# Moving the sample group's projections, attention and pooling from the first to the third group of a decoder step

## The reference, cut to what matters

```
z = x @ w_in                                  # pool 512 | q 512 | k 128 | v 128 | gates 2 x 1024
p_out, pool_state = pool_mixer(p, pool_prev, ...)   # windows 2, 4, 8, 16
o, k_state, v_state = attn(q, k, v)           # samples: kk = concat([ck, k]), vv = concat([cv, v])
m = g_pool * (p_out @ w_up_pool) + g_attn * (o @ w_up_attn)
x = layer_norm(alpha * x + m @ w_out)
idx, gate = top 16 of 128 x 128 experts, 8 heads    # product keys
x = layer_norm(alpha * x + sum_k gate_k * gelu(x . u[idx_k]) * v[idx_k])
```

## Time and profile before

| | |
|---|---|
| median of three runs | 3105.41 us (3104.44 to 3107.35) |
| the profiled execution | 3107.77 us, span 3105.9 us |
| busy, share of the span | PE 85%, DVE 74%, POOL 40%, ACT 31% |
| DMA | 1255.14 MB, mean 404 GB/s; q0 (gathers) 1107.36 MB, q1 (SP) 139.92 MB |
| chain that ended last | DMA 44%, PE 32%, DVE 16% |

### The profile page before, as it was taken

One profiled execution on the slowest core, in us unless ns is written; L12 is line 12 of the kernel. 1 busy time (PEld: TensorE's weight loads), 2 busy tenths in 40 slices (PEclk: granted clock), 3 DMA queues, 4 the chain that ended last, 5 costly groups with the idle time before them and its releaser, 6 DMA issues.

```text
span 3105.9 us, 31170 instructions
## 1 busy us (share of the span) xinstructions
PE 2643.5 (85%) x8204; PEld 1435.9 (46%) x8204; DVE 2297.3 (74%) x4977; ACT 955.6 (31%) x3100; POOL 1233.7 (40%) x1060
## 2 busy tenths in 40 slices
PE   8889999899998888999999879899877777676665
PEld 7866676555544444544444436434322222222222
DVE  2479668888866676888997676788878877666666
ACT  2124323333432232322444221433322322222222
POOL 0123433343443444334444444433454444544542
PEclk9989999999999999999999999999999998988988
DMA  9999999999999999999999999999999999999996
GB/s 284 250 414 417 384 417 419 419 419 419 420 420 418 420 408 412 411 402 414 404 408 380 418 420 420 421 420 418 419 421 421 421 421 422 421 421 422 421 421 259
DMA packets 203654, 1255.14 MB, mean 404 GB/s; under 512 B 31100, under 2 KB 34764, under 8 KB 67920
## 3 DMA queue, kind: packets, MB, share of 16 engines
q0 software_dynamic: 152064, 1107.36, 86.3%
q1 hardware_dynamic: 48656, 139.92, 12.5%
q10 hardware_dynamic: 2760, 5.88, 0.5%
HBM read 1247.39 MB, written 5.79 MB: 403 GB/s over the span
## 4 chain that ended last, share of the span: by engine, by line
DMA 44%; PE 32%; DVE 16%; issue 4%; ACT 2%; DVEq 1%; POOL 1%; ACTq 0%; POOLq 0%
DMA ring<-in_uv,idx 38%; PE acc L1103 15%; PE wide L1084 9%; DVE ring L1382 7%; DMA wring<-in_uv,idx 3%; PE wide L1301 3%; DVE acc_v L1393 2%; DMA wring<-in_w_q 2%; PE wide L1272 2%; DVEq L1366 1%; PE wide L1200 1%; DMA bias<-in_uv,idx 1%; POOL ring L848 1%; PE wide L1182 1%; ACT diag L893 1%
## 5 line engine op out<-in xcount | busy, mean ns | idle before, releaser
L848 POOL DMA_INDIRECT ring<-in_uv,idx x906 | 1054.3, 1164 | 1560.8 <-PE acc L1103 1044.8
L1103 PE MATMUL acc<-ring,diag 128*128 128x512 f32 (+1 forms) x2808 | 1373.1, 630 | 271.7 <-ACT diag L893 258.0
L1382 DVE CUSTOM_DVE_ANT_0 ring<-ring,xb 128x1024 f32<-128x1024 f32 x906 | 1097.0, 1225 | 469.5 <-DMA ring<-in_uv,idx 433.7
L1103 PEld LDWEIGHTS acc<-ring,diag 128*128 128x128 f32 (+1 forms) x2808 | 540.6, 199 | 975.2 <-issue 956.8
L879 ACT ACTIVATE hgelu<-hdot 128x2 f32<-128x2 f32 x528 | 107.2, 203 | 1723.3 <-DVE hdot L1382 1722.8
L1084 PE MATMUL wide<-xm,wring 128*128 128x256 f32 (+5 forms) x2352 | 608.6, 408 | 19.5 <-DMA wring<-in_w_q 18.4
L1084 PEld LDWEIGHTS wide<-xm,wring 128*128 128x128 f32 x2352 | 429.0, 197 | 214.0 <-issue 107.8
L893 ACT ACTIVATE diag<-ident,hw 128x128 f32<-128x128 f32 x813 | 294.3, 396 | 47.9 <-PE acc L1103 5.0
L1393 DVE SCALAR_TENSOR_TENSOR acc_v<-ring,hw,acc_v 128x1024 f32<-128x1024 f32 x204 | 262.1, 1285 | 38.2 <-ACT hw L882 17.9
L882 ACT ACTIVATE hw<-hgelu,gate 128x1 f32<-128x1 f32 x1056 | 253.6, 287 | 37.0 <-issue 0.7
L1301 PE MATMUL wide<-wring,big 128*128 128x256 f32 (+1 forms) x536 | 124.8, 379 | 0.0
(11 more groups left out here) (242 smaller groups left out, 1992.7 us busy)
## 6 DMA issues: line engine op xcount, KB each, us to landing
wring<-in_w_a SPq DMA_DIRECT2D x141, 512.0 KB, 7.9
wring<-in_w_q SPq DMA_DIRECT2D x64, 576.0 KB, 8.1
ring<-in_uv,idx POOLq DMA_INDIRECT x906, 20.7
ring<-in_w_a SPq DMA_DIRECT2D x27, 512.0 KB, 8.2
out_y_prompt<-xb ACTq DMA_DIRECT2D x7, 512.0 KB, 7.9
att<-in_ln_g SPq DMA_DIRECT2D x4, 512.0 KB, 12.1
att<-in_ln_b SPq DMA_DIRECT2D x4, 512.0 KB, 15.2
xm<-in_xT SPq DMA_DIRECT2D x1, 1536.0 KB, 10.5
```

What stands on the lines that cost most here:

```text
L848: pool.indirect_dma_start(slot(s), None, uv, bass.IndirectOffsetOnAxis(ap=idx[:, n % LISTS, j:j + 1], axis=0))\
L1103: k = mm(acc[0:width, c * 512:(c + 1) * 512], diag[:, r % DIAGS, 0:width], slot(s)[:, D + c * 512:D + (c + 1) * 512], start=(s == first), ...
L1382: V.tensor_tensor_reduce(u, u, x, 1.0, 0.0, ALU.mult, ALU.add, hdot[:, k, j:j + 1])\
```

## The change

The samples' columns leave the first group (144 columns in K and pool, 128 in q) and join the third group's (288 in place of 256 in its K, pool and q units; eight more matmuls in V). Their attention becomes a turn before the four of the third group. Two ring tiles, 0 and 1, leave the ring from slots 142 and 143 (`AWAY`) until slots 216 and 226 (`BACK`) and hold the samples' data. Their loads are issued by SP one or two at a time behind the weight loads of units 2 to 9 of the third group, their stores behind those of units 11 to 17. GpSimd holds slot 216 until the samples' values are multiplied, and slot 226 until all stores have landed. The mask is added into on VectorE in the third group, from a copy `sB` of the bias that stays in SBUF.

```diff
-    return SAMP if g <= WITH else 0
+    return SAMP if g == WITH else 0
...
-    return X0 if g in (0, WITH) else 0
+    return META if g == 0 else SAMP if g == WITH else 0
...
+AWAY = {tile: BATCH * int(CLOCKS[WITH].unit(POS_K) - 4) + tile for tile in (0, 1)}
+LEAVE.update(AWAY)
+BACK = {tile: BATCH * int(CLOCKS[WITH].attention(0, 0.0) + 14 - 5 * tile) for tile in (0, 1)}
...
+        if g == WITH:
+            put(pe, t.attention(-1, 0.02), 10.0, t.attention(-1, 0.96) - t.attention(-1, 0.02))
+            put(dve, t.unit(POS_Q) + 4.8, 5.0)
+            put(dve, t.attention(-1, 0.23), 5.0)
...
+            def load_samples(k):
+                if k == 0:
+                    for tile in BACK:
+                        wait_slot(sp, LAST_OF[tile], (slot_free, vslot_free))
+                if k < 2:
+                    for c in range(2 * k, 2 * k + 2):
+                        sp.dma_start(sPool[:, c, :, 0:PSTATE], stT[:, c]).then_inc(early_in, 16)
+                elif k == 2:
+                    sp.dma_start(sMask, smask_c).then_inc(early_in, 16)
+                    sp.dma_start(sSink, sink_rows).then_inc(early_in, 16)
+                elif k < 7:
+                    for s in range(2 * (k - 3), 2 * (k - 3) + 2):
+                        sp.dma_start(kX[:, s, 0:WIN], ckT[:, s, :]).then_inc(early_in, 16)
+                elif k == 7:
+                    sp.dma_start(vX, cv_rows).then_inc(early_in, 16)
...
-                    if g == 0 and pos == POS_QRY + 1:
-                        store_states()
+                    if g == WITH and pos <= POS_GATE:
+                        load_samples(pos - WR + 1)
+                    if g == WITH and POS_GATE + 1 <= pos <= POS_GATE + 7:
+                        store_states(pos - POS_GATE - 1)
...
+            def store_states(k):
+                if k == 0:
+                    sp.wait_ge(early_in, 15 * 16)
+                    sp.wait_ge(proj_evac, WITH * PROJ + POS_Q)
+                    sp.dma_start(k_sample, kX[:, :, DSEQ:DSEQ + WIN]).then_inc(early_out, 16)
+                elif k < 5:
+                    c = k - 1
                     sp.dma_start(pool_sample[:, c], sPool[:, c, :, DSEQ:DSEQ + PSTATE]).then_inc(early_out, 16)
...
-            for c in range(4):
-                sp.dma_start(sPool[:, c, :, 0:PSTATE], stT[:, c]).then_inc(early_in, 16)
-            sp.dma_start(sMask, smask_c).then_inc(early_in, 16)
-            sp.dma_start(sSink, sink_rows).then_inc(early_in, 16)
-            for s in range(SEQS):
-                sp.dma_start(kX[:, s, 0:WIN], ckT[:, s, :]).then_inc(early_in, 16)
-            sp.dma_start(vX, cv_rows).then_inc(early_in, 16)
...
-            pool.wait_ge(early_out, 16 * EARLY_STORES)
...
+                    if s == BACK_AT[1]:
+                        hold(pool, s_o, 1)
+                    if s == BACK_AT[0]:
+                        hold(pool, early_out, 16 * EARLY_STORES)
+                        hold(pool, pool_ready, WITH + 1)
...
                 if k:
                     act.wait_ge(o_ready, k)
+                if g == WITH and i == 0:
+                    act.wait_ge(s_o, 1)
...
                         if g == 0:
-                            parts += [(ps[0:SAMP, 256:384], META, X0), (ps[0:META, 384:512], 0, META)]
+                            parts += [(ps[0:META, 384:512], 0, META)]
+                        if g == WITH:
+                            parts += [(ps[0:SAMP, 256:384], 0, SAMP)]
...
-                if i == 0:
+                if g == WITH and i == 0:
+                    pe.wait_ge(s_o_evac, 8)
+                elif i == 0:
...
-                yield CLOCKS[0].attention(count, 0.02)
-                pe.wait_ge(sbias_sb, 1)
+                yield clock.attention(-1, 0.16)
                 pe.wait_ge(sq_ready, 1)
-                pe.wait_ge(max_ready, count)
+                pe.wait_ge(sc_evac, STEP0[WITH])
...
-                if g == 0:
-                    yield CLOCKS[0].attention(2, 0.47) + 1.0
+                if g == WITH:
+                    yield at + 0.8 * 4
+                    dve.wait_ge(early_in, 15 * 16)
```

More of the change, by code:

```diff
@@ L183, in __init__ @@
         blocks = SIZES[g] + (g == WITH)
-        turns = passes(g) + (g == 0)
+        turns = passes(g) + (g == WITH)
         cost = {}
         for pos in range(POS_GATE):
-            cost[pos] = n + (0 if g else X0 if pos < POS_Q else SAMP)
+            cost[pos] = wide if g else n + (META if pos < POS_Q else 0)
         for pos in range(POS_GATE, POS_UP):
@@ L353, in plan_sums @@
         for pos in range(POS_OUT):
-            put(pe, t.unit(pos), 8 * 0.0015 * (n if pos < POS_GATE else wide), 1.5)
+            put(pe, t.unit(pos), 8 * 0.0015 * wide, 1.5)
         for k in range(N_OUT):
@@ L481 @@
 TILE, USE, BEFORE = plan_ring()
+BACK_AT = {tile: TILE.index(tile, at) for tile, at in BACK.items()}
+LAST_OF = {tile: max(s for s in range(BACK[tile]) if TILE[s] == tile) for tile in BACK}
 def interleave(*parts):
@@ L830, in _ @@
                             hold(pool, idx_ready, part_count(n, k))
-                    if s == 1:
-                        hold(pool, s_o, 1)
                     if s == SPARE:
                         hold(pool, unit_done, POS_QRY)
-                    if BEFORE[s] is not None:
+                    if s == BACK_AT[1]:
[3 more added lines that the diff above has]
+                        hold(pool, pool_ready, WITH + 1)
+                    if s in BACK_AT.values():
+                        pass
+                    elif BEFORE[s] is not None:
                         if on_dve(BEFORE[s]):
@@ L1234, in sample_attention @@
                         rows = slice(HD * kv, HD * kv + HD)
-                        out = acc[rows, pair * 32:pair * 32 + 32]
+                        out = wide[0][rows, pair * 32:pair * 32 + 32]
                         for n in range(2):
@@ L1564, in sample_attention @@
             def sample_attention():
-                count = passes(0)
-                yield CLOCKS[0].attention(1, 0.28) + 0.1
-                dve.wait_ge(proj_evac, POS_GATE)
+                clock = CLOCKS[WITH]
+                yield clock.attention(-1, 0.06)
+                dve.wait_ge(early_in, 15 * 16)
+                for t in range(2):
+                    for n in range(2):
+                        mask = sMask[:, t, n * WIN:(n + 1) * WIN]
+                        V.tensor_tensor(mask, sB[:, 0:WIN], mask, ALU.add)
+                    mask = sMask[:, t, 256:288].rearrange("p (s i) -> p s i", s=SEQS)
+                    V.tensor_tensor(mask, sB[:, WIN:WIN + DSEQ].unsqueeze(1).to_broadcast([P, SEQS, DSEQ]), mask, ALU.add)
+                dve.wait_ge(proj_evac, WITH * PROJ + POS_GATE)
                 for s in range(SEQS):
@@ L1833 @@
     xs = a["x_sample"].reshape(SAMP, D)
-    extra = np.concatenate([a["meta_tokens"], xs], axis=0)
+    extra = [a["meta_tokens"] if g == 0 else xs if g == WITH else xs[:0] for g in range(GROUPS)]
     xT = np.zeros((GROUPS, P, DC * COLS), np.float32)
     for g in range(GROUPS):
-        part = np.concatenate([extra[X0 - x0(g):], x[FIRST[g] * P:(FIRST[g] + SIZES[g]) * P]], axis=0)
+        part = np.concatenate([extra[g], x[FIRST[g] * P:(FIRST[g] + SIZES[g]) * P]], axis=0)
         xT[g, :, 0:part.shape[0] * DC] = part.reshape(-1, DC, P).transpose(2, 1, 0).reshape(P, -1)
```

126 lines of the change are left out of this document (59 added, 67 removed).

## The result

The changed kernel takes 3113.99 us (median of 11 executions, 3112.20 to 3119.83); the kernel before, run beside it on the same chip, 3105.91 us (11 executions, 3102.39 to 3110.06). The ratio is 1.0027, with a 95% interval of 1.0019 to 1.0035: slower by some 8.4 us. The profiled execution of the change took 3114.56 us, its span 3112.8 us. Lines of the change are those of the second listing of orders above (`L1126` projections, `L1143` the sums of slots, `L1165` the mirror product, `L883` the gathers).

What follows compares the result with a forecast made beforehand. It took the DMA engines as full from the first gather on, TensorE limiting the front. -6.3 - 2.8 + 12.8 + 9 + 7 = +19.7 us on the profiled 3107.8 gave 3127.5, stated as 3125 us for the median; range 3098 to 3150.

Steps and rivals of the forecast that it cites:

- What bounds the kernel: TensorE limits the front; from the first gather on the DMA engines are full, share 1.00 to 1.02.
- Rival 2: Third group: TensorE binds there, not DMA, so the moved traffic costs nothing; faster, 3096 us, chance 0.13.
- The front, -6.3: Front: with fewer columns the first gather comes 6.3 us earlier, the bias windows' load limiting the gain; bounds 5.3 and 8.4.
- Query loads, -2.8: Front: two more query units land before the first gather, gaining 2.8 us; bounds 0 and 2.8.
- Traffic in full DMA time, +12.8: Third group: the moved sample loads and stores cost 12.8 us of full DMA time; from 5.7 to 27.
- The wait for unit 3's weights, +9: Third group: weights behind 2048 small runs make TensorE wait some 25 us, emptying the gathers' queue; +9 us, bounds 0 and 25.
- The wait at the stores, +7: Third group's gate units: stores of 1024 runs delay weights, one gap of 11 us less 4; +7 us, bounds 0 and 36.
- Edits at nothing: Third group: sample work, holds, the ring's two missing tiles and SP's issue time were costed at nothing.
- Rival 1: Third group: small runs do not hold the weights up, only front and DMA time count; 3109 us, chance 0.27.

Runs made afterwards that it cites:

- the variant with few runs: The change with pool states loaded and stored as 128 runs a time through a compact stage, key store cut into four of 256 runs; 3101.48 us, ratio 0.9978.
- its two halves: The change with only the pool-state loads compact, 3107.64 us, and the change with only the stores compact and spread, 3108.24 us; ratio 1.0004 each.
- stores spread: The change with its seven groups of stores behind every second unit, ring tile 0 back 22 batches later; 3110.50 us, ratio 1.0014.
- few runs in the front: The kernel before, its pool states in the front loaded and stored as one transfer of 128 runs each through a compact stage; 3104.86 us, ratio 0.9999.

## Why the prediction was wrong

The direction was right, and so was the mechanism; the size was not: some 8 us slower in place of the 19.6 that 3125 stands above the median shown. The forecast's sum was +19.7, the trace's own is +8.3 at the gather of slot 1050.

- **What bounds the kernel: right.** Without the traffic the third group takes as long as before, to within 3 us, with TensorE's added work in it. Rival 2, by which TensorE binds there and traffic is free, falls: in the variant with few runs 2.3 MB cost 6.9 us with no wait for weights left.
- **The front, -6.3: right.** -6.4, and the mirror product waits for the bias windows as the step said. One term ahead of that wait was too large: the removed block of V matmuls was put at 1.85 us and gave 0.94, and TensorE was ready 1.82 us earlier in place of 3.0. It did no harm, since the bias load sets that point.
- **Query loads, -2.8: too small.** Seven query loads are issued before the first gather in place of five, the two more that were counted, but slot 0 to 128 is 6.3 us shorter. In the six other kernels of the same front and ring (few runs, its two halves, loads from ScalarE's queue, stores spread, no traffic) it is 396.2 to 399.5 us; the two others with the old front (without two tiles, few runs in the front) have 401.2 and 400.9. The means of the two sorts are 4.1 us apart, so some 2 us of the 6.3 are the spread between executions. The gain is there early: slot 16 leaves 35.0 to 38.7 us behind the first gather with the new front, 40.6 to 44.1 with the old one. TensorE's wait for `w_q` fell from 15.8 only to 13.4. The small stores in the old front are not the cause; what the rest is stays open.
- **Traffic in full DMA time, +12.8: about right.** 14.5 us more on q1, 3.5 less on q0, 11.0 together. The forecast had nothing for q0, so that the sum comes this near is in part luck. The term for the runs, on top of 5.7 for the bytes, is borne out: with few runs q1 costs 7.5 more than before, with many 14.5.
- **The wait for unit 3's weights, +9: mechanism right, size off.** The pace of q1 was taken as 40 packets a microsecond from the earlier trace rows, whatever the packets' size. In rows 10 q1 had a packet for 480 of q0's 683, so it was not always waiting for a turn. In rows 11 it nearly always was, 409 for 425, but its packets were 4 KB and took 33.9% of the engines' time, so that each pair of turns lasted longer; 660 of 60 bytes took 3.9%. With such runs always waiting the pace is that of q0, 660 packets in 12 us, 55 a microsecond. So the 2048 runs needed some 37 us, not 51, and TensorE waited 12.6 us, not 25. The empty queue lasted about as long as said (from within 664 to 668 until within 676 to 680 us), but cost 6.1 us.
- **The wait at the stores, +7: the step that failed most.** The same pace makes a store and its weights 1152 / 55 = 21 us in place of 28 (by the prediction's own 40 it is 28.8), so the shortage was 5 x 21 - 60 - 24 = 21 us and not 56. The wait was 22.2 - 12.6 = 9.6 us, and nearly all of it was covered by gathers under way: 2.2 us of empty time. That cover depends on how many gathers are under way at that moment: with the loads from ScalarE's queue a wait of 10.1 us there left 8.1 us empty. Together the two gaps cost 8.2 us where 16 were forecast, 7.8 of the 11.4 us by which the sum was too high; the query loads are 3.5 more, the traffic 1.8 and the later groups -1.8.
- **Edits at nothing.** The tiles, the sample work and the holds cost nothing, or 3 us at most, in the third group, as said. That SP's own issue time lies where it would wait for a buffer was wrong: with the runs in q1, SP itself was held, 21.94 us for one pair of state loads, so the weights behind them were not even issued before 666.03 us. That did not add to the wait at 668 us, which was for weights issued earlier.
- **Rival 1, small runs do not hold weights up** (0.27), gave 3109 us, nearer to the measured time than the forecast, for a reason that the trace refutes. Weights behind 2048 runs landed after 36.5 us in place of 8. The Trainium skill, "DMA: Bandwidth & Descriptors", section "Queues, rings and completion order", has an engine drain a packet of some 9 to 17 descriptors before it turns to the next queue. By that, an estimate from the page's figure at 55 turns a microsecond, some 500 to 900 small runs a microsecond would have gone through, if a gathered row is a turn of its own. The trace does not agree: 660 packets of q1 beside 660 of q0, and 0.04 MB in them, so 60 bytes, one run, for a turn, one after the other.

## What to carry to other kernels

Count a queue's packets, not only its bytes: beside a full queue of gathers each run took one turn here, and whatever stood behind it in its queue waited for all those turns. So work that is moved from idle DMA time into full DMA time should go with its short runs joined into long ones first, by a copy on an engine with time to spare; here that turned +0.27% into -0.22%. And where two costs are forecast for the same stretch, a wait and the traffic that goes through during it, look whether one pays for the other before adding them.

## What the runs showed that was not expected

- **Turns are even to the packet while both queues have work.** 660 for 660 in 12 us; from 644 to 656 us, when q0's share is 92.1%, q1 gets 904 for 621. DMA of the change by queue from 760 to 776 us, at the stores, shows the same:

```profile
q0 software_dynamic: 843, 6.14, 91.1%
q1 hardware_dynamic: 843, 0.57, 11.0%
```

- **Runs that wait in a queue also hold the engine that issues to it.** An issue that took 0.33 to 0.45 us elsewhere held SP 9.80 us for weights and 21.94 us for two state loads; in the variant with few runs the same weights took 0.33 us at 631.70; at the stores, in SP's timeline, weights took up to 18.20 us to issue:

```profile
758.97 14.38 SPq L752 DMA_DIRECT2D wring<-in_w_a  x1
773.39 2.14 SPq L818 DMA_DIRECT2D out_pool_sample<-ring  x1
775.58 18.20 SPq L752 DMA_DIRECT2D wring<-in_w_a  x1
```

- **A wait costs clock too.** Behind TensorE's idle 12.6 us the granted clock stood at 0.50, 1.2 GHz, from 664 to 668 us, and the same eight recorded matmuls took 4.18 us at 668.64 and 2.10 at 676.66, when it was 1.00, 2.4 GHz, again.
- **The ring's tiles are worth different times in different groups.** Two of them cost nothing that shows in the third group and some 6 us in the second, by the dot products (8.5 by the gathers).
